# Turning laid among the next block's products, and attention slots that open with their own turning

## The reference

```python
proj = rms_norm(x, norm1) @ w_in                 # 1576 columns: u, q, k, v, qi, ki, wi, qm
q, k = rope(rms_norm(q)), rope(rms_norm(k))      # 8 query heads, 2 key heads, 64 wide
qi, ki = rope(qi) * 32 ** -0.5, rope(ki)         # 8 indexer heads and one key, 32 wide
score = einsum('bth,bths->bts', wi, relu(qi . ki))   # visible keys only (chunks of 64 rows)
keep the top k = min(256, L / 4) keys of each row; softmax(q . k) @ v over the kept keys
softmax(qm . mem_k) @ mem_v                      # 4 memory heads, 256 memory rows
a_pool = trailing means of u (2, 4, 8, 16 rows) minus u, a linear map, a scale
h = x + concat(a_pool, a_attn, a_mem) @ w_out; up-projection, convolution, gate, down-projection
```

## Time and profile before

| | us |
|---|---|
| runs | 3462.66, 3463.76, 3467.8 (median 3463.76) |
| profiled execution | 3470.27 |
| its span, first to last instruction | 3468.5 |
| TensorE busy in the span | 3047.9 (88%) |
| VectorE, ScalarE, GpSimd busy | 2096.3, 1117.9, 1271.5 |
| mean granted TensorE clock | 0.942 |

### The profile page before, as it was taken

How to read it: one execution, slowest core, us unless ns; L and a number is a source line. 1 busy time by engine, 2 the same in 40 slices (tenths; PEclk the granted TensorE clock), 3 DMA queues, 4 the chain that set the end, 5 groups by cost and what they waited for, 6 DMA issues and landing times. The chain is left out here.

```text
span 3468.5 us, 49639 instructions
## 1 busy us (share of the span) xinstructions
PE 3047.9 (88%) x18810; PEld 2837.3 (82%) x18810; DVE 2096.3 (60%) x3980; ACT 1117.9 (32%) x1932; POOL 1271.5 (37%) x478
## 2 busy tenths in 40 slices
PE   3899995677788878979899999999698999999997
PEld 2677773566677767869799999999697999999996
DVE  4566663577777767732376666665414766676664
ACT  2222221466676756642212111211212122112211
POOL 0000000457778867104453334332135433344320
PEclk7899996689999989999899999999898999999998
DMA  3122224322121110104211111110222111111101
GB/s 126 63 100 85 82 78 134 86 58 59 36 52 36 30 27 24 37 22 131 67 55 55 36 36 50 59 36 24 103 78 67 49 60 37 36 48 56 41 12 51
DMA packets 164903, 201.54 MB, mean 58 GB/s; under 512 B 27903, under 2 KB 138788, under 8 KB 162724
## 3 DMA queue, kind: packets, MB, share of 16 engines
q1 hardware_dynamic: 164772, 199.87, 18.2%
HBM read 154.58 MB, written 45.25 MB: 58 GB/s over the span
## 5 line engine op out<-in xcount | busy, mean ns | idle before, releaser
L907 POOL TENSOR_TENSOR att_relu<-att_relu,keep_w 128x2048 f32<-128x2048 f32 (+12 forms) x84 | 257.6, 3067 | 799.9 <-ACT att_relu L1062 799.4
L1724 DVE SCALAR_TENSOR_TENSOR ffn_gv<-ffn_up,ffn_taps,ffn_gv 128x1056 f32<-128x1056 f32 (+2 forms) x264 | 417.7, 1596 | 143.1 <-ACT ffn_gv L1677 136.8
L1617 PE MATMUL ffn_ps_u<-feed_nhi,feed_up_hi 128*128 128x352 f32 x2112 | 459.6, 326 | 16.2 <-DVE feed_nlo L1755 11.4
L1745 DVE TENSOR_TENSOR feed_hT<-feed_hT,ffn_ps_d 128x352 f32<-128x352 f32 x528 | 275.1, 521 | 328.1 <-PE ffn_ps_d L1630 328.1
L1617 PE MATMUL ffn_ps_u<-feed_nhi,feed_up_lo 128*128 128x352 f32 x2112 | 456.5, 324 | 0.0
L1617 PE MATMUL ffn_ps_u<-feed_nlo,feed_up_hi 128*128 128x352 f32 x2112 | 455.8, 324 | 0.0
L1617 PEld LDWEIGHTS ffn_ps_u<-feed_nhi,feed_up_hi 128*128 128x128 f32 x2112 | 360.8, 190 | 20.0 <-DVE feed_nlo L1755 13.1
L1630 PE MATMUL ffn_ps_d<-ffn_a_hi,ffn_down_hi 128*128 128x352 f32 x1056 | 343.4, 325 | 29.3 <-DVE ffn_a_lo L1736 24.0
L1617 PEld LDWEIGHTS ffn_ps_u<-feed_nhi,feed_up_lo 128*128 128x128 f32 x2112 | 363.5, 188 | 0.0
L1617 PEld LDWEIGHTS ffn_ps_u<-feed_nlo,feed_up_hi 128*128 128x128 f32 x2112 | 359.8, 188 | 0.0
L1008 PEld LDWEIGHTS att_ps_o<-att_v,att_pT 128*128 128x128 f32 x2176 | 282.9, 196 | 89.2 <-ACT att_pT L835 83.8
(11 more groups left out here) (254 smaller groups left out, 5996.9 us busy)
## 6 DMA issues: line engine op xcount, KB each, us to landing
feed_raw_up<-in_w_up SPq DMA_DIRECT2D x44, 1024.0 KB, 4.9
scratch_sT<-proj_sT SPq DMA_DIRECT2D x16, 1472.0 KB, 5.1
ffn_raw_down<-in_w_down SPq DMA_DIRECT2D x22, 1024.0 KB, 4.8
feed_nlo<-scratch_mixT SPq DMA_DIRECT2D x16, 528.0 KB, 7.9
proj_x<-in_x_prompt SPq DMA_DIRECT2D x16, 512.0 KB, 4.7
att_qi<-scratch_sT SPq DMA_DIRECT2D x16, 512.0 KB, 3.5
att_qa<-scratch_sT SPq DMA_DIRECT2D x16, 512.0 KB, 5.0
att_qb<-scratch_sT SPq DMA_DIRECT2D x32, 256.0 KB, 5.6
```

What stands on the lines that cost most here:

```text
L907: st.step(pool.tensor_tensor(at, at, weights, ALU.mult))
L1617: ins = pe.matmul(ps_u[:, half, s, 0:SUB], a[:, q, k, :], b[:, k, SUB * s:SUB * s + SUB], start=(k == 0 and n == 0), stop=(k == KC - 1 and ...
L1724: ins = dve.scalar_tensor_tensor(gv[:, half, lo:hi], up[:, lo + shift + j - 2:hi + shift + j - 2], taps[:, 2 * j + half, e:e + 1], gv[:, h ...
L1745: dve.tensor_tensor(at, at, ps_d[:, j % 2, 0:SUB], ALU.add).then_inc(partial_read[j % 2], 1)
```

## The change

In the projection the six head groups of block n are turned by TensorE inside the last column group of block n+1's products (two groups before each of the matmuls c = 0, 3, 6), and ScalarE alone copies them (`place_heads`, ahead of its last scaling). The pool scaling and the copy to `u_old` go from VectorE to ScalarE (`place_pool`); `square` moves into `scale`, ahead of the second group; `root` comes before `turn`. VectorE waits, before it overwrites `stack`, until the previous block is turned. The sample block is turned in `mix_pool`, behind the others.

In attention a slot opens with the transposes of its own first two groups; the logits of slot i+2 and the first raw score follow, then the value matmuls. The previous block's rows are turned after the value matmuls of head 0, and ScalarE copies them after that head's groups; the numbers of the groups are shifted to match. Raw scores, relus and weighings of blocks 0 and 1 are gone, and with them VectorE's waits before their masks. The loads change order: queries of block 0, keys and values of blocks 0 to 2 (`FIRST`), score queries of block 2, all score keys, queries of block 1, the other keys and values, score queries of block 3, the sample's keys, tables.

```diff
             def pair(i):
                 for u in range(2):
                     call(0, 2 * i + u + 1, 1 - u, i + u)
                     call(1, 2 * i + u, u, i)
+                    call(4, 2 * i + u + 2, u, i + 1)
                     call(2, 2 * i + u + 2, u, i + 1)
                     call(3, 2 * i + u, u, i)
-                    call(4, 2 * i + u + 2, u, i + 1)
...
             def store_turned(n, u, T, i):
-                sp.wait_ge(read_act, 4 * n + 4)
-                sp.wait_ge(read_dve, 4 * n + 4)
+                sp.wait_ge(read_act, N_T * (n + 1))
...
                 for g, (a, b) in enumerate(GROUPS):
+                    if g == 1 and not (isinstance(n, int) and n == NB):
+                        square(n + 1, 1 - u, TS if isinstance(n, int) and n + 1 == NB else P, i + u)
+                    if g == 3 and not (isinstance(n, int) and n == 0):
+                        place_heads(n - 1, P)
                     act.wait_ge(product, 4 * n + g + 1)
...
-            def place(n, u, T, i):
+            def place_heads(n, T):
                 act.wait_ge(turned_stored, 32 * n)
-                for g in (0, 2, 4):
+                for g in range(6):
+                    k = min(4, NSLOT - 4 * g)
                     act.wait_ge(turned, N_T * n + g + 1)
...
+                    act.activation(sT[:, 4 * g:4 * g + k, 0:T], src, ACT.Copy).then_inc(read_act, 1)
+
+            def place_pool(n, u, T, i):
+                if T == TS:
+                    place_heads(n, T)
                 act.wait_ge(turned, N_T * n + 7)
                 act.activation(zT[:, :, 0:T], ps_t[:, 0, 0:256].rearrange("p (s n) -> p s n", n=P)[:, :, 0:T], ACT.Copy).then_inc(read_act, 1)
+                if T == P:
+                    act.activation(u_old[96:P, :], pr[96:P, u, U0:Q0], ACT.Copy).then_inc(old_ready, 1)
+                act.wait_ge(turned, N_T * n + 8)
+                for c in range(2):
+                    ins = act.activation(poolT[:, c, 0:T], ps_t[:, 1, P * c:P * c + T], ACT.Identity, scale=keep["pool_scale"][:, c:c + 1])
+                ins.then_inc(read_act, 1)
...
                     for c in range(KC):
+                        if g == 3 and c % 3 == 0 and not (isinstance(n, int) and n == 0):
+                            turn_heads(n - 1, 1 - u, P, 2 * (c // 3))
...
+            def turn_heads(n, u, T, start):
+                if start == 0:
+                    pe.wait_ge(prepared, n + 1)
...
+                for g in (start, start + 1):
+                    pe.wait_ge(read_act, N_T * n + (g - 1 if g >= 2 else 0))
                     for s in range(min(4, NSLOT - 4 * g)):
                         ins = pe.transpose(ps_t[:, g % 2, P * s:P * s + T], stack[0:T, 4 * g + s, :].bitcast(F32), ident[0:T, 0:T])
                     ins.then_inc(turned, 1)
-                pe.wait_ge(read_act, 4 * n + 3)
+
+            def mix_pool(n, u, T, i):
+                if T == TS:
+                    for start in (0, 2, 4):
+                        turn_heads(n, u, T, start)
+                pe.wait_ge(read_act, N_T * n + 5)
                 pe.wait_ge(old_ready, n + 1)
...
                 dve.tensor_scalar(w_at, row[:, WI0:QM0], (IH * ID) ** -0.5, None, ALU.mult).then_inc(heads_ready, 1)
+                if not (isinstance(n, int) and n == 0):
+                    dve.wait_ge(turned, N_T * n - 2)
...
-            def place(n, u, T, i):
-
-                dve.wait_ge(turned_stored, 32 * n)
-                src = ps_t[:, 1, :].rearrange("p (s n) -> p s n", n=P)[:, :, 0:T]
-                for g in (1, 3, 5):
...
+            def load_keys(lo, hi, loaded):
+                for j in range(NKV):
+                    sp.dma_start(kT[:, j, P * lo:P * hi].rearrange("p (n w) -> p n w", w=P).bitcast(F32), sT[SLOT_K + j, :, lo:hi]).then_inc(loaded, 16)
+                sp.dma_start(v[:, lo:hi, :], new_v[:, lo:hi, :]).then_inc(loaded, 16)
...
             load(BLOCKS[0])
+            load_keys(0, FIRST, first_keys)
+            load_index(2)
+            sp.dma_start(kiT[:, :].rearrange("p (n w) -> p n w", w=P).bitcast(F32), sT[SLOT_KI, :, 0:NB]).then_inc(index_keys_loaded, 16)
+            load(BLOCKS[1])
+            load_keys(FIRST, NB, keys_loaded)
+            load_index(3)
+            load_sample()
...
-            load(BLOCKS[1])
-            load_index(2)
-            load_index(3)
...
-            for b in BLOCKS:
+            for b in BLOCKS[2:]:
                 for s, (lo, hi) in enumerate(b.segs):
                     first_four, last_four = weigh(b, s, 0), weigh(b, s, 1)
...
                 for g in range(min(2, len(groups))):
                     turn(g)
+                if later:
+                    early_logits(*later)
+                index_pieces(other, numbers[0:1])
                 for g in range(len(groups)):
...
-            for b in BLOCKS[0:2]:
-                index_pieces(b, range(IH * len(b.segs)))
-            pe.wait_ge(keys_loaded, 16 * KEY_LOADS)
             for slot in range(-INDEX_LEAD, 0):
                 index_pieces(*index_share(slot))
-            for first_heads in heads[0:2]:
-                early_logits(*first_heads)
             for i, b, h, _, later in slots():
-                if later:
-                    early_logits(*later)
                 other, numbers = index_share(i)
-                index_pieces(other, numbers[0:1])
+                head_values(b, h, other, numbers, later)
                 if h == 0 and b.n:
                     rows_turned(BLOCKS[b.n - 1])
-                head_values(b, h, other, numbers[1:], later)
...
-                if h == 0 and b.n:
-                    copy_groups(act, BLOCKS[b.n - 1], 9)
                 other, numbers = index_share(i)
...
                 copy_groups(act, b, h, relu_next, (lambda: exponentials(*after)) if after else None)
+                if h == 0 and b.n:
+                    copy_groups(act, BLOCKS[b.n - 1], 9)
```

More of the change, by code:

```diff
@@ L493, in square, with first_square @@
                 act.activation(junk[0:T, :], x[0:T, u, :], ACT.Square, accum_out=ss[0:T, u:u + 1]).then_inc(squares, 1)
+            def first_square(n, u, T, i):
+                if isinstance(n, int) and n == 0:
+                    square(n, u, T, i)
             def scale(n, u, T, i):
@@ L537, in product_of @@
                     ins.then_inc(product, 1)
[L539 to L547, removed]
-                        pe.wait_ge((read_act, read_dve)[g % 2], 4 * n)
+            def turn_heads(n, u, T, start):
+                if start == 0:
+                    pe.wait_ge(prepared, n + 1)
+                    if isinstance(n, int) and n == 0:
+                        pe.wait_ge(consts, 16 * NCONST)
+                for g in (start, start + 1):
+                    pe.wait_ge(read_act, N_T * n + (g - 1 if g >= 2 else 0))
                     for s in range(min(4, NSLOT - 4 * g)):
@@ L641, in prepare @@
                 split_index(dve, st, stack[0:T, SLOT_KI:SLOT_KI + 1, :], qi[:, 8:9, :], key=True, signal=prepared)
[L643 to L658 removed]
+            pipeline(prepare=prepare, turn=turn, root=rms, weights=split_weights, loop=dve.Fori, steps=st)
 def segments(width):
@@ L750, in phase_attend @@
             units_before.append(units_before[-1] + NH * len(b.units) + 1)
-            groups_before.append(groups_before[-1] + NH * len(b.groups) + 4)
+            groups_before.append(groups_before[-1] + NH * len(b.groups) + (4 if b.n else 2))
         def group_index(b, h, g):
-            return groups_before[b.n] + (h * len(b.groups) + g if h <= NH else NH * len(b.groups) + 2 + g)
+            if h > NH:
+                return groups_before[b.n + 1] + (0 if b.sample else len(BLOCKS[b.n + 1].groups)) + g
+            return groups_before[b.n] + h * len(b.groups) + g + (2 if h and b.n else 0)
         def bank_reads(index):
@@ L902, in weigh @@
                 w = b.segs[s][1] - b.segs[s][0]
-                group = 2 * (segs_before[b.n] + s) + half
+                group = 2 * (index_segs(b) + s) + half
                 at = relu[0:b.T, group % RING, :, 0:w]
@@ L1054, in index_relu @@
                 for piece in pieces:
-                    i, s = IH * segs_before[b.n] + piece, piece // IH
+                    i, s = IH * index_segs(b) + piece, piece // IH
                     lo, hi = b.segs[s]
@@ L1082, in exponentials @@
                 ins.then_inc(exp_done, 1)
-            for b in BLOCKS[0:2]:
-                index_relu(b, range(IH * len(b.segs)))
             for slot in range(-INDEX_LEAD, 0):
@@ L1113, in pick @@
                 col = lambda x, i=0: x[0:T, i:i + 1]
-                if part == 0:
-                    dve.wait_ge(seg_kept, segs_before[b.n + 1])
+                if part == 0 and b.keep:
+                    dve.wait_ge(seg_kept, index_segs(b) + len(b.segs))
                     dve.wait_ge(tables_loaded, 16 * TABLE_LOADS)
@@ L1119, in pick @@
                         st.step(dve.memset(at, 0.0))
```

(3 more changed lines are left out.)

75 lines of the change are left out of this document (33 added, 42 removed).

## The result

The changed kernel takes 3402.19 us (median of 4 runs, 3398.78 to 3404.97) against 3464.85 us (4 runs) of the kernel before on the same chip: ratio 0.9818, 95% interval 0.9801 to 0.9835. That is 63 us faster and 37 us short of the 99 that the sum gave: inside the range that also took in the rivals (3325 to 3415), 12 us outside the forecast's own (3330 to 3390). The profiled execution took 3404.97 us (span 3403.2, clock 0.946), 65.3 us less than that of before. The feed stage gives nothing of it: the last block's rows are divided 65.2 us earlier than before, and the span ends 65.3 us earlier.

A forecast was written before the change was run, and what follows sets the result against it. TensorE was taken to bound the projection, loads the start of attention, and handshakes the slots. Gains of 41 + 22 + 36 = 99 us gave 3371 us against the profiled execution, 3365 as median; own range 3330 to 3390, with rivals 3325 to 3415.

The forecast's parts named there:

- the 99 that the sum gave: Whole kernel: gains of 41 us in projection, 22 at attention's start and 36 in its slots, added up.
- the rivals: Whole kernel: five other outcomes, at 3401, 3403, 3405, 3527 and 3464 us, chances 0.18, 0.08, 0.05, 0.04 and 0.03.
- Part 1: Projection: turning heads among the next block's products saves 41 us, bounds 34 and 46.
- Part 2: Start of attention: fewer bytes loaded ahead of slot 0 save 22 us, bounds 15 and 26.
- Part 3: Attention slots: own turnings first and previous rows later save 36 us, bounds 0 and 79.
- The half taken for blocks 1 to 3 (16): Attention, 27 slots: half of 31 us of logits and raw scores put under copy and exponential, 16 us gained.
- The 20 for the later blocks: Attention after 760 us: 20 us gained for all these blocks, chiefly at their starts.
- the row wait: Attention: TensorE's 30.9 us wait for the previous block's last rows; turnings inside it save 13 times 0.87, or 11 us.
- The forecast's warning sign: Attention: ScalarE's idle before the second copy as large as what the first gained would show the forecast wrong.
- Slots give nothing: Attention slots: VectorE's one-by-one steps and the moved raw score stay, no slot gain, 3401 us; chance 0.18.
- The clock falls oftener: Attention, 760 to 1516 us: slow clock for a third of the blocks costs about 40 us, 3405; chance 0.05.
- Logits behind the turnings: Attention: VectorE's mask starts 0.87 us later in each of 144 slots, +125 us, 3527; chance 0.04.

The follow-up runs named there:

- e8: The kernel of e4 with each head slot turned twice in place among the projection's products: 3427.36 us, one execution.
- e2: The changed kernel with the old order in a slot and the old place of the previous block's rows: 3409.52 us.
- e3: The changed kernel with slot 1's logits issued before the previous block's rows and the own probabilities are turned: 3403.97 us.
- e5: The kernel of e4 with ScalarE making slot 0's sign sum before it copies the previous block's rows: 3398.68 us.
- e6: The kernel of e4 with the edits of both e3 and e5: 3388.50 us.
- e9: The kernel of e4 where, from block 3 on, only slot 0 opens with its own turning; other slots have logits and first raw score ahead: 3387.07 us.
- e10: The kernel of e9 with ScalarE making slot 0's sign sum before it copies the previous block's rows: 3379.62 us.
- e11: The kernel of e9, but slot 1 too opens as in the changed kernel (rows, own turning, then logits): 3380.46 us.
- e4: The changed kernel with the map of a block's pool rows moved into the first column group of the products after next: 3382.95 us.

## Why the prediction was right, and where it fell short

The range holds because it was made wide enough for the rivals; the forecast itself, with 0.62 the likeliest case, missed by 37 us. Two of its three parts fell short, one by its clock and one by its overlap.

**Part 1, forecast 41, measured 32.7.** Its other steps hold. 23 turnings and six changes of kind cost 263.43 - 258.06 - 2.84 = 2.53 us in the last group (the group took 270.73 - 267.89 = 2.84 in the earlier trace rows), so a change costs next to nothing where 0.3 were taken, and an undisturbed period is 24.85, not 25.1. Copies and preparation kept their cover. The sample's preparation starts at 519.49, 0.5 us behind its products, where 1.0 was taken. Missing is the clock: the 15 periods from block 1 to block 16 take 382.64 us, and 15 x 24.85 would be 372.75, so half-speed products cost 9.9, of which block 1's 1.5 were there before. The step that failed is a term put at nothing: the sum left the projection at the clock of 1.00 that the earlier trace rows shows. Its ground, that turning did not bring the clock down, is true of turnings, as e8 shows; but behind the stretch that keeps the pool mixing the clock now falls, and that the periods before passed the same matmuls at 1.00 was no surety for the changed one. The Trainium skill, "TensorE: Matmul & The Clock Gate", Part 4: PE-mode transpose, has the fast clock not engage for transposes. e8 does not agree for turnings laid among matmuls: it has twice the turnings and a mean clock of 1.00 over 425 us.

**Part 2, forecast 22, measured 20.0 to slot 0.** The first turning comes 18.6 us after the first load (17 forecast), the selection of block 2 at 584.02 - 547.73 = 36.3 us after it (617 - 580.46 = 36.5 forecast); the 1.5 us that the sum took for landing stand in no row. The one wait for block 3's score queries is 3.58 us, below the 5 that would have counted as wrong.

**Part 3, forecast 36, measured 7.** This is the term that was mis-sized; e2 puts it at 7 us. The half taken for blocks 1 to 3 (16) was too much by a factor of two: 11.6 us of lead in blocks 0 to 2, of which e2, without the slot edits, shows 3.7 (one execution each). The 20 for the later blocks did come, at their starts as forecast, and went again: slot 0 is 1.25 us shorter in the mean and slot 1 1.4 us longer. The step that failed is the overlap: that 0.87 us of turnings run inside the row wait are 0.87 us saved in each of 13 blocks. Slot 0's own turning does run there now, and head 1's exponential comes 1.8 us earlier, but the sign sum behind it does not (7.76 us against 7.79). The rows' turning, placed at the end of slot 0, stands with its copies before that sign sum, before slot 1's own turning and before the logits of head 3. e3, e5, e6, e9 and e10 each put one or two of these three in front; the others then came later, and slots 0 and 1 together took between 16.70 and 18.13 us in every kernel, 16.83 before. Which single wait sets these two slots stays open. The forecast's warning sign, ScalarE's idle before the second copy as large as what the first gained, is there in part: before the relus, which stand ahead of the second copies, it idles 92 us more, against 140 less before copies.

**The rivals.** "Slots give nothing", 3401, is nearest, and right for the blocks from 3 on; that its number comes within 1.2 us is luck, since the first two parts gave 10 us less than it took and what lies behind slot 0's start 12.5 us more. "The clock falls oftener" happened, at a quarter of its price and in the other stage. "Logits behind the turnings" is real in slot 6 (0.47 us, gone in e9 to e11) and in slot 0 (0.5 us), not in every slot; it does not decide. The waits of value matmuls for copies, to be cut to a third in blocks 0 to 5, fell there from 28.0 to 16.6 us only, while those for VectorE's division rose from 10.2 to 26.3.

## What to carry to other kernels

Work laid among matmuls of another stage costs its bare duration, here 0.109 us a turning, and it is then worth asking what is left between the products, not only what was moved in: behind the 4 us that stayed there the clock fell, 10 us over the stage, and moving one small step of them (e4) gave 19 us. A wait that disappears from a list by name is not gained before the next slot's time shows it: compare leads slot by slot, and where one slot gains what the next one loses, look for the marker that did not move, here the second sign sum; several queues met there, and none of the reorderings tried on e4 paid more than some 3 us. A sum of waits is an upper bound and little more when another engine works step by step: of 79 us here 7 came.

## What the runs showed that was not expected

The clock of TensorE fell to half for 3.7 us in nearly every second period, after a stretch in which it was busy 3.5 of 4.0 us with the pool's matmuls, and it did not in the kernel before, where a 10 us stretch held the same matmuls. With the map moved out it did not fall from block 2 on; with the mixing doubled and no idle time it fell in nine of the 14 from there on. Why the fall comes in some periods and not in others is open, and so is what separates the mixing from the turnings: the shapes differ (128*64 and 32*64 in the rows against 128*128), eight turnings of x stand right ahead of the mixing in every period, and neither was varied by itself.
